# A streaming encoder step with expert retrieval: packed sample rows, finer merge steps, and waiting sums at the head of TensorE's steps

## The reference

```python
n = rms_norm(x, norm_mix);  proj = n @ w_in            # q, k, v of two attentions, forget gate, two gates
o_fox = fox_attention(...); o_sb = stick_breaking_attention(...)     # 8 heads of 64 each
h = x + (sigmoid(ga) * (o_fox @ w_o_fox) + sigmoid(gb) * (o_sb @ w_o_sb)) @ w_out
# PEER: for each row x of rms_norm(h): 8 heads, top 16 of 128 keys in two halves, top 16 of the 256 pairs
w   = softmax(score) * gelu(expert_u[e] . x)           # 128 experts e per row
out = h + sum over the 128 experts of w * expert_v[e]
```

## Time and profile before

| | us |
|---|---|
| runs (3) | 4946.55, 4955.14, 4979.13; median 4955.14 |
| profiled execution | 4956.09, with a span of 4954.3 |
| mean granted TensorE clock | 0.791 of full speed |
| PE busy | 3632.0 (73%) |
| DVE busy | 2923.7 (59%) |
| POOL busy | 1526.2 (31%) |
| ACT busy | 1247.9 (25%) |
| DMA | 1331.43 MB, 269 GB/s in the mean; POOL's gathers and stores 1142.48 MB |

### The profile page before, as it was taken

How to read it: one execution, slowest core, us unless ns; L and a number is a source line. 1 busy time by engine, 2 the same in 40 slices (tenths; PEclk the granted TensorE clock), 3 DMA queues, 4 the chain that set the end, 5 groups by cost and what they waited for, 6 DMA issues and landing times.

```text
span 4954.3 us, 33835 instructions
## 1 busy us (share of the span) xinstructions
PE 3632.0 (73%) x10298; PEld 1799.4 (36%) x10298; DVE 2923.7 (59%) x5665; ACT 1247.9 (25%) x2721; POOL 1526.2 (31%) x1309
## 2 busy tenths in 40 slices
PE   6799996488946777873688877637776776266698
PEld 4344443344533443452344444414432334122221
DVE  2300001577596777569676765876566657966786
ACT  1111102155113444110344421123434311011010
POOL 0111000034222444332243333312223333255554
PEclk9999996678976877986687788867667888677655
DMA  3212113489947998995799899747778898499743
GB/s 115 73 54 91 70 52 104 176 332 375 361 187 283 393 384 351 403 382 204 285 379 353 325 385 398 301 181 292 296 287 315 327 391 364 188 393 420 261 123 97
DMA packets 252050, 1331.43 MB, mean 269 GB/s; under 512 B 30968, under 2 KB 74232, under 8 KB 105408
## 3 DMA queue, kind: packets, MB, share of 16 engines
q0 software_dynamic: 164768, 1142.48, 58.8%
q1 hardware_dynamic: 87104, 186.80, 10.5%
HBM read 1294.07 MB, written 35.10 MB: 268 GB/s over the span
## 4 chain that ended last, share of the span: by engine, by line
PE 32%; DVE 21%; DMA 17%; ACT 6%; issue 5%; POOL 2%; SPq 2%; DVEq 0%; ACTq 0%; POOLq 0%
PE pv L821 17%; DMA uv<-expert_uv,rows_u 13%; DVE uv L1181 6%; PE pb L802 4%; PE pb L893 3%; PE pb L773 3%; PE pb L919 2%; DMA arena<-out_sv_p 2%; PE pb L869 2%; POOL uv L730 2%; DVE arena L1171 2%; SPq L660 2%; DVE acc L1207 1%; DVE arena L1259 1%; DVE arena L1251 1%
## 5 line engine op out<-in xcount | busy, mean ns | idle before, releaser
L730 POOL DMA_INDIRECT uv<-expert_uv,rows_u x1152 | 1436.0, 1247 | 2715.2 <-PE pv L821 1555.1
L821 PE MATMUL pv<-uv,diag 128*128 128x512 f32 (+1 forms) x2880 | 1701.4, 754 | 609.8 <-ACT diag L1025 541.0
L1181 DVE CUSTOM_DVE_ANT_0 uv<-uv,nr 128x1024 f32<-128x1024 f32 (+1 forms) x1152 | 1366.2, 1219 | 558.6 <-DMA uv<-expert_uv,rows_u 556.6
L821 PEld LDWEIGHTS pv<-uv,diag 128*128 128x128 f32 (+1 forms) x2880 | 628.9, 226 | 1565.6 <-issue 1484.3
L248 PE MATMUL ps<-win,xg 128*128 128x512 f32 (+1 forms) x1440 | 631.1, 597 | 0.0
L773 PE MATMUL pb<-arena 64*128 64x512 f32 (+6 forms) x544 | 280.7, 623 | 381.4 <-DMA arena<-out_sv_p 189.2
L1207 DVE SCALAR_TENSOR_TENSOR acc<-uv,wgt,acc 128x1024 f32<-128x1024 f32 (+1 forms) x423 | 542.8, 1283 | 14.7
L1033 ACT ACTIVATE gel<-dots 128x4 f32<-128x4 f32 (+1 forms) x288 | 59.1, 205 | 1791.8 <-DVE dots L1181 1791.7
L248 PEld LDWEIGHTS ps<-win,xg 128*128 128x128 f32 (+1 forms) x1440 | 261.1, 184 | 343.1 <-issue 342.9
L802 PE MATMUL pb<-arena 128*128 128x64 f32 (+3 forms) x1728 | 318.4, 346 | 45.9 <-ACT o L1012 45.7
L1025 ACT ACTIVATE diag<-ident,wgt 128x128 f32<-128x128 f32 (+1 forms) x720 | 239.7, 383 | 397.5 <-DVE wgt L1193 299.7
(11 more groups left out here) (156 smaller groups left out, 2516.8 us busy)
## 6 DMA issues: line engine op xcount, KB each, us to landing
arena<-w_stream SPq DMA_DIRECT2D x80, 1024.0 KB, 9.2
win<-w_main SPq DMA_DIRECT2D x10, 2048.0 KB, 9.0
uv<-expert_uv,rows_u POOLq DMA_INDIRECT x1152, 9.8
scratch_gates<-stage POOLq DMA_DIRECT2D x32, 256.0 KB, 2.3
arena<-scratch_gates SPq DMA_DIRECT2D x8, 1024.0 KB, 24.8
xg<-x_t SPq DMA_DIRECT2D x8, 536.0 KB, 7.7
arena<-scratch_c_p SPq DMA_DIRECT2D x8, 520.0 KB, 11.7
xr<-x SPq DMA_DIRECT2D x8, 512.0 KB, 4.3
```

The source lines that it names most:

```text
L730: pool.indirect_dma_start(out=uv[k % NU][0:r].rearrange("p a n -> p (a n)"), out_offset=None, in_=io["expert_uv"][:, :], in_offset=bass.In ...
L821: mm = nc.tensor.matmul(pv[0:r, c * BANK:(c + 1) * BANK], diag[n % ND][0:r, 0:r], uv[k % NU][0:r, 1, c * BANK:(c + 1) * BANK], start=n == ...
L1181: nc.vector.tensor_tensor_reduce(out=u, in0=u, in1=nr[t % 3][0:r], scale=1.0, scalar=0.0, op0=ALU.mult, op1=ALU.add, accum_out=dots[b % 2] ...
```

## The change

**Packed samples.** Tile 8's 128 slots of 32 rows become 32 slots of 128 partitions: partition group i (32 partitions) holds experts 32 i to 32 i + 31 of the 32 samples. SP makes the packed numbers, weights and four copies of the normed rows by twelve small DMAs; POOL waits for them before slot 1024. At the end DVE adds `pv` to the held sums, PE adds the four groups by a matmul with `sel`, and DVE adds that to h. There are 1056 slots in place of 1152, and 40 lots after the last merge, all of 128 rows.

**Finer steps.** A merge of two tiles has 28 steps in place of 18: each pick of halves stands in its own step, and each choice of experts is cut in five. The 64 lots of waves 2 to 4 thus spread over 60 steps: 34 in attend, 30 in merge; four steps get two lots.

**Order.** PE sums lot b-1 at the head of the step (`in_front`). DVE does its own work, then `dot(b)` and `weigh(b)`. ACT keeps its order. `close` moves from a tile's second lot to its first. The bodies of the merge functions are otherwise the same.

```diff
-            steps = [("attend", g, s) for s in range(self.end[g] - self.first[g])] + [("merge", g, s) for s in range(MERGE_STEPS)]
+            steps = [("attend", g, s) for s in range(self.end[g] - self.first[g])]
+            steps += [("merge", g, s) for s in range(len(merge_steps(self.tiles[g])))]
             first, count = self.tiles[g - 1][0] * LOTS, len(self.tiles[g - 1]) * LOTS
             for i, step in enumerate(steps):
                 self.lots[step] = range(first + i * count // len(steps), first + (i + 1) * count // len(steps))
-        self.rest = range(self.tiles[-1][0] * LOTS, (self.tiles[-1][-1] + 1) * LOTS)
+        self.rest = range(self.tiles[-1][0] * LOTS, ALL_SLOTS // LOT)
 
     def on_dve(self, k):
         j = k % NK
         return j % LOT == 0 or (j % LOT == 1 and j // LOT % 2 == 1)
 
 
-MERGE_STEPS = 18
+def merge_steps(tiles):
+
+
+    steps = [("outputs",), ("y", 0), ("y", 1), ("merged",), ("h", 0), ("h", 1), ("norm",), ("turned",)]
+    picks = [(hp, ti) for hp in range(PAIRS) for ti in range(len(tiles))]
+    for h in range(HEADS):
+        ready = [x for x in picks[:1] if x[0] < h // 2]
+        steps.append(("queries", h, ready[0] if ready else None))
+        picks = picks[len(ready):]
+    steps += [("halves", x) for x in picks]
+    return steps + [("experts", ti, part) for ti in range(len(tiles)) for part in range(EXPERT_PARTS)]
+
+
+EXPERT_PARTS = 5
+ALL_SLOTS = (TILES - 1) * NK + NK // 4
+
+
+def tile_of(k):
+    return min(k // NK, TILES - 1)
+
+
+def slots_to(t):
+
+    return (t + 1) * NK if t < TILES - 1 else ALL_SLOTS
...
+        def normed_row(t):
+
+            return nr[t % 3] if t < TILES - 1 else nr[TILES % 3]
+
+        def slot_index(k):
+            t, j = tile_of(k), k - tile_of(k) * NK
+            return rows_u[:, t % 4, j:j + 1] if t < TILES - 1 else rows_pk[:, j:j + 1]
+
+        def lot_gates(b):
+            t, j = tile_of(b * LOT), b * LOT - tile_of(b * LOT) * NK
+            return gw[:, t % 4, j:j + LOT] if t < TILES - 1 else gw_pk[:, j:j + LOT]
...
+                t = TILES - 1
+                sp.wait_ge(named, TILES)
+                sp.wait_ge(dotted, slots_to(TILES - 3))
+                for i in range(4):
+                    part, cols = slice(i * NS, (i + 1) * NS), slice(i * NS, (i + 1) * NS)
+                    sp.dma_start(rows_pk[part, :], rows_u[0:NS, t % 4, cols]).then_inc(packed, 16)
+                    sp.dma_start(gw_pk[part, :], gw[0:NS, t % 4, cols]).then_inc(packed, 16)
+                    sp.dma_start(normed_row(t)[part, :], nr[t % 3][0:NS, :]).then_inc(packed, 16)
...
+                        if t < TILES - 1:
+                            pool.wait_ge(named, t + 1)
+                        else:
+                            pool.wait_ge(packed, 16 * 12)
...
-                def beside(step):
-                    for b in plan.lots.get(step, ()):
+                def fold():
+
+                    pe.wait_ge(sel_made, 1)
+                    pe.wait_ge(closed, TILES)
+                    for c in range(2):
+                        mm = nc.tensor.matmul(pb[0:NS, c, :], sel[:], held[(TILES - 1) % 2][:, c * BANK:(c + 1) * BANK], start=True, stop=True)
+                    mm.then_inc(folded, 1)
+
+                def in_front(step):
+                    for b in list(plan.lots.get(step, ()))[:1]:
                         if b:
                             background(b - 1)
+
+                def behind(step):
+                    for b in list(plan.lots.get(step, ()))[1:]:
+                        background(b - 1)
 
                 def attend(g):
                     n0, units = plan.first[g], plan.end[g] - plan.first[g]
                     for s in range(-2, units + 2):
+                        if 0 <= s < units:
+                            in_front(("attend", g, s))
                         turns = len(plan.turns[n0 + s - 1]) if 0 < s <= units else 0
                         for i in range(turns):
                             turn(n0 + s - 1, i)
@@ -838,7 +900,7 @@
                         if 2 <= s:
                             values(n0 + s - 2)
                         if 0 <= s < units:
-                            beside(("attend", g, s))
+                            behind(("attend", g, s))
...
+                    for s, step in enumerate(merge_steps(tiles)):
+                        in_front(("merge", g, s))
+                        if step[0] == "outputs":
+                            turn_outputs()
+                        elif step[0] == "y":
+                            project_outputs(step[1])
+                        elif step[0] == "merged":
+                            turn_merged()
+                        elif step[0] == "h":
+                            project_merged(step[1])
+                        elif step[0] == "turned":
+                            turn_normed()
+                        elif step[0] == "queries":
+                            h = step[1]
+                            queries(h)
+                            if h:
+                                scores_of(h - 1)
+                            if h == HEADS - 1:
+                                scores_of(h)
+                        behind(("merge", g, s))
...
+                fold()
...
-                    if b % LOTS == 1 and t:
+                    if b * LOT == t * NK and t:
...
+                def close_samples():
+                    t = TILES - 1
+                    row = held[t % 2]
+                    dve.wait_ge(valued, pe_slots[ALL_SLOTS])
+                    dve.wait_ge(summed, dve_slots[ALL_SLOTS])
+                    nc.vector.tensor_tensor(row[:], row[:], pv[:], ALU.add).then_inc(closed, 1)
+                    dve.wait_ge(h_in, 16 * TILES)
+                    dve.wait_ge(folded, 1)
+                    nc.vector.tensor_tensor(hb[0:NS].rearrange("p (c n) -> p c n", c=2), hb[0:NS].rearrange("p (c n) -> p c n", c=2),
+                                            pb[0:NS, 0:2, :], ALU.add).then_inc(ended, 1)
+
+                def lots(step):
+                    for b in plan.lots.get(step, ()):
                         dot(b)
-
-                def behind(step):
-                    for i, b in enumerate(plan.lots.get(step, ())):
-                        if i:
-                            dot(b)
                         weigh(b)
 
                 def attend(g):
@@ -1238,8 +1314,7 @@
                         if 0 <= s + 1 < units:
                             exponents(n0 + s + 1)
                         if inside:
-                            ahead(("attend", g, s))
-                            behind(("attend", g, s))
+                            lots(("attend", g, s))
...
+                    for s, name in enumerate(merge_steps(tiles)):
+                        if name[0] == "y":
+                            merge_rows(name[1])
+                        elif name[0] == "h":
+                            add_rows(name[1])
+                        elif name[0] == "norm":
+                            norm()
+                        elif name[0] == "queries" and name[2]:
+                            pick_halves(g, *name[2])
+                        elif name[0] == "halves":
+                            pick_halves(g, *name[1])
+                        elif name[0] == "experts":
+                            pick_experts(tiles[name[1]], name[1], name[2])
+                        lots(("merge", g, s))
```

More of the change, by code:

```diff
@@ L523, in stream @@
         nr = [sb(f"nr{i}", [P, D]) for i in range(3)]
-        acc = [sb(f"acc{i}", [P, D]) for i in range(2)]
+        held = [sb(f"held{i}", [P, D]) for i in range(2)]
         hb = sb("hb", [P, D])
@@ L1032, in gelus @@
                         act.wait_ge(weighted, b - 1)
-                    nc.scalar.activation(gel[b % 2][0:r, :], dots[b % 2][0:r, :], ACT.Gelu).then_inc(gelu, 1)
+                    nc.scalar.activation(gel[b % 2][:], dots[b % 2][:], ACT.Gelu).then_inc(gelu, 1)
                 def ahead(step):
@@ L1067, in merge @@
                     width = sum(query_rows(t) for t in tiles)
-                    at = lambda s: ("merge", g, s)
-                    ahead(at(0))
-                    for ti, t in enumerate(tiles):
-                        r = query_rows(t)
-                        act.wait_ge(o_turned, t + 1)
-                        nc.scalar.activation(ot[:, :, ti * P:ti * P + r], pturn[:, :, 0:r], ACT.Copy).then_inc(ot_out, 1)
-                    behind(at(0))
-                    for s in (1, 2):
-                        ahead(at(s))
-                        behind(at(s))
@@ L1099, in merge, with take_outputs @@
[L1099 to L1107 removed]
+                    def take_outputs():
+                        for ti, t in enumerate(tiles):
+                            r = query_rows(t)
+                            act.wait_ge(o_turned, t + 1)
+                            nc.scalar.activation(ot[:, :, ti * P:ti * P + r], pturn[:, :, 0:r], ACT.Copy).then_inc(ot_out, 1)
@@ L1218, in close @@
```

(48 more changed lines are left out.)

332 lines of the change are left out of this document (154 added, 178 removed).

## The result

The changed kernel takes 5206.75 us (median of 4 runs, 5202.09 to 5210.04) against 4952.66 us for the kernel before (4946.55 to 4979.13): a ratio of 1.050, 95% interval 1.046 to 1.054, slower. Its profiled execution took 5210.04 us with a span of 5208.3. In the following, waves are cut as in the earlier trace rows: from a wave's first unit to the first turning of its outputs (attention), from there to the last expert numbers (merge).

The account below looks back on a forecast made before the run. It took DMA to bound tile 7's full lots, PE tile 8's 32-row lots, and no engine to be full in the waves. 4956.1 + 134 (attention) + 252 (merges) - 196 (packing) = 5146, predicted 5145 us, range 4690 to 5290.

Parts of the forecast that it names:

- the serial case: Whole kernel: PE's sums, turn, exponents and weighing run in series; slower, 5145 us, own range 4955 to 5385, chance 0.62.
- Packing, -196: Stage after the last merge: 8 full lots replace 32 lots of 32 rows, 196 us less, between 190 and 200.
- rival D: Packing doesn't pay because POOL's wait for `packed` stalls a full pipeline, needing over 190 us; given no chance.
- Sums at the head, in attention: Sums delay turn and exponents: waves 2 to 4 take 543, 609, 675 us against 492, 545, 666; wave 1 +10.
- The lots that leave: Attention has seven lots fewer in each of three waves; double steps there, nine before and two after.
- A: Waits hide: waves keep their time, packing alone counts, 4760 us, or 4690 without PE's waits for `ended`; chance 0.20.
- +134: Attention of all four waves: total 134 us longer, although seven lots fewer in each of three waves.
- Finer steps, +252 in the merges: Merges: more lots in the DVE-bound expert choice, +72 us each in waves 2 to 4, +36 in wave 1.
- I let the two cancel: 0: First 16 merge steps: savings from leaving lots offset a 27 us series; 0, between -25 and +25 a wave.
- B: Half of the loss hides as DVE catches up and the first 16 merge steps quicken: 4953 us, chance 0.12.
- C: Gathers start 10 us earlier everywhere and merges reach attention's 0.9 DMA share: 4570 us, chance 0.06.
- "wrong" signs: Wave 2's attention under 492 us or merges under 400 refute the serial chain; last stage over 480, the packing's price.

Follow-up runs that it names:

- turn first: The changed kernel with PE's turn of the previous unit moved ahead of the lot's sums in attention, merges unchanged: 4790.6 us, ratio 0.967.
- the mixtures: The changed kernel with sums ahead of PE's turn only before kind 0 units (4879.6 us) or only before kind 1 units (5048.93 us), behind it in other steps.
- sums behind everywhere: The changed kernel with PE's sums behind its own work in every step and `close` back in the tile's second lot: 4672.64 us, ratio 0.943.
- packing only: The kernel before with the packed samples alone, steps and orders as before: 4774.09 us, ratio 0.964.
- Dots ahead in the merges: Changed kernel, turn ahead of sums in attention, a merge step's first dot ahead of DVE's own work: 4582.61 us with merge sums behind, 4679.34 in front.

## Why the prediction was right

Forecast 5145, slower, by the serial case; measured 5206.75 against it, so 62 us too low in sum, inside the range. By its steps:

- **Packing, -196.** The last stage fell by 199 us in the changed kernel and 189 alone, at 384 and 371 GB/s. Right, and with packing alone every stage of the waves is within 8 us of before, so rival D falls. What it said beside this of the earlier `close` was wrong: PE's waits for `ended` did not go, they take 76.6 us in the changed kernel (DVE `hb`, line 1290) against 68.8 before, and the sum counted no such wait.
- **Sums at the head, in attention.** Predicted 543, 609 and 675 for waves 2 to 4, measured 564, 599 and 660; a kind 1 step of wave 2 18.7 predicted, 20.5 in the rows above. The chain named (sums, turn, `turn_out`, magnitudes, exponents) is shown by turn first, where one move takes 416 us away, and by the mixtures. In wave 1 +10 was predicted and +49 measured: the argument that its sums wait for nothing new failed. ACT makes a lot's diagonals only in the step of the next lot, so PE at its head waits for them here too (33.2 us in 16 steps, with turn first 3.7 in 2), and ACT waits 111.9 us for the turn.
- **The lots that leave.** The text on the kernel before gives 41 of 64 lots to attention and 23 to the merge. The rule that spreads them (32 x 64 / 50, rounded down) gives 40 and 24, so six lots leave each attention and not seven, and the double steps there are eight and not nine. The first 16 merge steps had 21 lots and not 20. The serial sum doesn't use the count before; A's 74 us a wave would be 63.
- **+134 was a net sum.** The price of the order is 384 us in attention; the +165 measured over before (+134 predicted) is that less the lots that left (-212 by sums behind against packing only) and what packing moved. The prediction's working built whole steps with the lots that they then hold, so it has both terms in it; that +134 lies near +165 rests on this and on luck, as waves 1 and 2 were 39 and 20 us too low, waves 3 and 4 12 and 16 too high.
- **Finer steps, +252 in the merges.** The total was near (+287), and its first term was right: the expert choice of wave 2 (from the copy of the key numbers, line 1356, to the last expert numbers) takes 74 us before and 130 after, and 130 with the sums behind too. That is 56 us for eight of the ten lots more (two stand with the last picks of halves), 7.0 a lot against the 7.2 of the sum.
- **"I let the two cancel: 0"** is the step that held by luck: cut as the prediction cuts it, it came out at +13, +13, +12 and -3 us in waves 1 to 4, as the difference of two larger terms. From wave 2's first turning to its expert choice the trace has 295 us before, 273 with sums behind everywhere, and 323 after. So the fewer lots and finer steps save 22, and the order of PE costs 50: the prediction wrote down a series of 27 us in such a step and set it against lots that leave. In all, the merges cost +113 us with the sums behind (some 32 of them from DVE's dots behind, by "Dots ahead in the merges") and +172 more from the sums in front.
- **Rivals.** A ("the waits hide", 4690 to 4760) is false for the changed kernel and nearly true without its order: sums behind everywhere gives 4672.64, 17 us under it. Its reason is not shown: wave 2's attention has a DMA share of 0.91 there, but DVE waits 14.0 us for gathers and 90.5 for the magnitudes. B and C did not happen; what C hoped of early sums, more DMA in attention, came only with the turn ahead.
- **Signs.** Right: PE waits for diagonals 32 times in wave 2's attention, the exponents' wait there grew from 71.8 to 161.1 us, DVE's wait for gathers fell to 98.2 us, the DMA share is 0.72 to 0.75 in attention, waves 2 to 4 take 1017, 1051 and 1097 us against 985, 1050 and 1115. None of the "wrong" signs appeared.

The best kernel run has packing, finer steps, the turn ahead of the sums, the merges' sums behind, and dots ahead: 4582.61 us, 7.4% below the kernel before and 12% below the changed one.

## What to carry to other kernels

Work that fills waiting time on an in-order engine goes behind the last instruction that another engine reads in that step, and ahead of the rest; find that instruction by following the longest wait of each engine back once around, and price what is put ahead of it at its full length in every step. Put at the right place, earlier sums do free buffers somewhat earlier (19 and 21 us in the attention of two waves here); at the head they turn a wait for data into a wait for each other, and the sign is that busy times fall while the stage grows. Look at every instruction that stands behind the delayed one on the next engine: here the magnitudes were one and the gelu another. A change of several parts needs each part alone and in pairs: packing gained some 185 us, finer steps with DVE's new order some 100, PE's order cost 534, and about half of what that cost in the merges was there only beside DVE's new order.

## What the runs showed of the hardware

TensorE's granted clock in wave 2's attention was 0.79 before, 0.72 after, 0.81 with turn first, a mixture of the levels 1.2 and 2.4 GHz. The lowest goes with the most idle time of PE: 206 of 563 us, against 118 of 492 before and 99 of 424 with turn first. PE's waits for diagonals do not order the three: they are 162.8 us after, 9.6 before and 72.0 with turn first. By the Trainium skill (TensorE: Matmul & The Clock Gate, "What's actually happening") only activity takes the array out of its throttled state; these three stages agree. The last 295 us of the earlier trace rows do not: PE is busy for 273 us there, with sums of 32 rows, and the granted clock is 0.50, the level of 1.2 GHz. The term is the smaller part of the loss: the 348 sum matmuls of wave 2's attention take 235.0 us after and 204.8 with turn first, 30 of the 140 us between the two stages. A single short wait decides nothing: after the 1.96 us wait above the sums took 0.59 us each (7.03 for 12), and in the earlier trace rows 0.59 straight behind PE's own work (7.11 for 12) and 0.46 after a wait of 1.90 us (3.67 for 8).

One core drew 384 GB/s over the last 446 us, at a DMA share of 0.94. The Trainium skill (DMA: Bandwidth & Descriptors, "Where 436 GB/s comes from") says that for transfers between HBM and SBUF the HBM side binds at about 358; with one core at work this run exceeds that by 7%.
